# VectorE's order in attention, two moves on TensorE, and the last update in halves, in a two-layer hybrid decoder

## The chip, the cores and the metric

The kernel runs on 1 core of one Trainium2 chip. The time is device microseconds of one launch, the median of several runs. The engines of the core are TensorE (PE, with its weight loads PEld), VectorE (DVE), ScalarE (ACT), GpSimd (POOL) and SyncE (SP), which here issues all DMAs.

## What is computed

Two layers on 256 tokens of width 1024, float32. Each layer projects its normalised input into queries, keys and values for two groups of heads. Group SWA is sliding-window attention with sinks (8 query heads, 2 key/value heads, window 128), group MOBA is, at 256 tokens, plain causal attention (8 heads). A feed-forward part follows.

```python
def hybrid_layer(x, cos, sin, w_in, b_in, w_out, ...):
    h = rms_norm(x, g_attn_pre)
    proj = jnp.einsum('bsd,de->bse', h, w_in) + b_in
    mq, mk, mv, sq, sk, sv = jnp.split(proj, SPLIT_OFFSETS, axis=-1)
    ...
    mo = rms_norm(moba_attention(mq, mk, mv).reshape(b, s, MOBA_WIDTH), g_moba_out)
    so = rms_norm(swa_sink_attention(sq, sk, sv, sinks).reshape(b, s, SWA_WIDTH), g_swa_out)
    mix = jnp.concatenate([mo, so], axis=-1)
    x = x + rms_norm(jnp.einsum('bse,ed->bsd', mix, w_out), g_attn_post)
    h = rms_norm(x, g_ffn_pre)
    f = jax.nn.silu(jnp.einsum('bsd,df->bsf', h, w_gate)) * jnp.einsum('bsd,df->bsf', h, w_up)
    x = x + rms_norm(jnp.einsum('bsf,fd->bsd', f, w_down), g_ffn_post)
    return x
```

Queries and keys of both groups are rotated (`apply_rope`) between projection and attention.

## The kernel before

**Tiles.** The 256 tokens are two tiles of 128 rows, t = 0 and 1. Weights come in blocks of 1 MB (128 x 2048 float32) into three `raw` buffers. Each float32 product is made of three matmuls: every operand is split into a high part and a low part, and PE adds high x high, high x low and low x high. For each block b, ScalarE writes the high part (`hi`, L500), and VectorE the low part (`lo`, L703), a subtraction that reads the raw block and the high part, both in SBUF: 128 x 2048 elements. `after(L, b)` stands for the parts of the block that takes the place of block b: `after(L, 0)` is `lo` of block 4, `after(L, 1)` of block 5, and so on.

**Projections.** Blocks 0 to 8 are the input projection in five column groups, ci = 0 (SWA keys and values, block 0), 1 (SWA queries, blocks 1 and 2), 2 (MOBA keys, blocks 3 and 4), 3 (MOBA queries, 5 and 6), 4 (MOBA values, 7 and 8). On PE, `multiply(L, t, b)` is one block's matmuls for tile t, and `multiply(L, t, b, (0,))` the first half of them. `project(L, ci, t)` on VectorE (L747, for ci = 0 also L745) takes the sum out of its PSUM bank, scales it and adds the bias, into `stage[t]`.

**Rotation.** `rotate(L, ci, t)` on POOL makes six instructions (L422 to L427) of 128 x 256 elements (128 x 64 for ci = 0) that read `stage[t]` and write `roped[t]`. Then `qk(L, ci, t)` on PE transposes `roped[t]` (L1013), and ScalarE keeps the result (`keep_qk`). `roped[t]` exists once for each tile, so a rotation waits for the transposes of the one before on the same tile:

```python
                if ci:
                    b = BANK_OF["qk", ci - 1, t]
                    pool.wait_ge(full[b], HELD[b].done(L, ("qk", ci - 1, t)))
```

POOL does the rotations in the order (0,0), (1,0), (0,1), (1,1), (2,0), (2,1), (3,0), (3,1), with the small steps of a norm between the last ones.

**Attention** runs in three rounds for each group: `scores` (PE, L1038), `maxima` (VectorE, L766 to L775), `exps` (ScalarE), `probs_transposed` (PE, L1013), `keep_probsT` (half on ScalarE, half on VectorE, L788), `values` (PE, L1063), and `normalise` (VectorE, L797 to L799).

**Order.** Every engine has its own program, one list of calls in a fixed order, and the engines meet only through semaphores. On PE the matmuls of the projections lie between the steps of attention, so that PE has work while other engines do theirs. An engine that waits for one step holds up all that stands behind it in its list.

**The end.** In the last layer `update_x(L, 1, 1)` (VectorE, L827) adds the feed-forward result to `x` for tile 1, over all 1024 columns, and SP then stores the tile with one DMA (L367).

Of the kernel before, what the change touches and what calls it, by code (L numbers as in the profile page):

```python
# [22 lines left out]
ALU = mybir.AluOpType  # L23
# [4 lines left out]
T = 2  # L28
# [7 lines left out]
BANK = 512  # L36
# [3 lines left out]
MOBA, SWA = 0, 1  # L40
# [114 lines left out]
BANK_OF = {name: b for b in range(8) for name in HOLDS[b]}  # L155


def trunk(nc, x_in, w_in, b_in, w_out, g_attn_pre, g_attn_post, g_moba, g_swa, sinks_in,
# [4 lines left out]
    with ExitStack() as ctx:  # L163
# [3 lines left out]
        def sem(name):  # L167
            return ctx.enter_context(nc.semaphore(name))
# [76 lines left out]
        rstd_o_ready = sem("rstd_o_ready")  # L245
        o_scaled = sem("o_scaled")
        eps_added = sem("eps_added")
        pool_step = sem("pool_step")
        dve_step = sem("dve_step")

# [28 lines left out]
        def tokens(t):  # L279
            return slice(t * P, (t + 1) * P)  # L280
# [8 lines left out]
        def _(sp):  # L289
# [40 lines left out]
            for L in range(depth):  # L330
# [23 lines left out]
                if L < depth - 1:  # L354
# [7 lines left out]
                    load_sinks(following)  # L362
                    for b in range(RAW + 1):
                        load_block(following, b)
            for t in range(T):
                sp.wait_ge(x_ready, X_READY.done(depth - 1, (1, t)))
                sp.dma_start(out[0, tokens(t), :], x[:, t, :]).then_inc(out_done, 16)  # L367
            sp.wait_ge(out_done, 16 * T)


        @block.gpsimd
# [318 lines left out]
        def _(dve):  # L690
# [15 lines left out]
            def after(L, b):  # L706
                for c in freed_by(b):
                    lo(L, c)
# [114 lines left out]
            def update_x(L, ph, t):  # L823
# [4 lines left out]
                                               x[:, t, :], ALU.mult, ALU.add).then_inc(x_ready, 1)  # L828
                X_READY.tick((ph, t))

            def swiglu(L, c, t):
                n = min(BANK, FF - c * BANK)
                b = BANK_OF["up", c, t]
                dve.wait_ge(full[b], HELD[b].done(L, ("up", c, t)))
                bg = BANK_OF["gate", c, t]
                dve.wait_ge(drained[bg], HELD[bg].done(L, ("gate", c, t)) + 1)
                if c:
                    bt = BANK_OF["ft", c - 1, t]
                    dve.wait_ge(full[bt], HELD[bt].done(L, ("ft", c - 1, t)))
                nc.vector.scalar_tensor_tensor(f[t][:, 0:n], bank[b][:, 0:n], rstd_x[:, t:t + 1], silu[t][:, 0:n],  # L840
                                               ALU.mult, ALU.mult).then_inc(drained[b], 1)
# [10 lines left out]
            for L in range(depth):  # L852
# [4 lines left out]
                loT(L, ("ht", 0, 1, 1))  # L857
                project(L, 0, 1)
                after(L, 0)
                after(L, 1)  # L860
                maxima(L, SWA, 0)
                project(L, 1, 1)
                after(L, 2)
                keep_probsT(L, SWA, 0)
                after(L, 3)
                project(L, 2, 0)
                normalise(L, SWA, 0)
                project(L, 2, 1)
                maxima(L, SWA, 1)
# [3 lines left out]
                maxima(L, SWA, 2)  # L873
                scale_o(L, SWA, 0)
                keep_probsT(L, SWA, 2)
                after(L, 5)
                project(L, 3, 1)
                after(L, 6)
                normalise(L, SWA, 1)
                maxima(L, MOBA, 0)  # L880
# [64 lines left out]
                    lo(L + 1, 1)  # L945
                    lo(L + 1, 2)
                scale_y(L, 1, 1)
                update_x(L, 1, 1)
                if L < depth - 1:
                    dve.wait_ge(x_ready, X_READY.done(L, (1, 1)))  # L950
                    scale_rows(L + 1, 0, 1)
                assert n_step[0] == (L + 1) * PER_LAYER, n_step
# [3 lines left out]
        def _(pe):  # L956
# [59 lines left out]
            def rows(L, ph, t):  # L1016
                pe.wait_ge(rows_ready, ROWS.done(L, (ph, t)))
                for half in range(2):
                    transpose(L, ("ht", ph, t, half), lambda q: y[t][:, half, q * P:(q + 1) * P], 4)
# [66 lines left out]
            for L in range(depth):  # L1086
# [2 lines left out]
                multiply(L, 0, 1)  # L1089
                multiply(L, 0, 2)  # L1090
                rows(L, 0, 1)
                qk(L, 0, 0)
                multiply(L, 0, 3)
                rows_landed(L, 0, 1)
                multiply(L, 1, 0)
                qk(L, 1, 0)
# [27 lines left out]
                probs_transposed(L, SWA, 2, 0)  # L1124
                probs_transposed(L, SWA, 2, 1)
                multiply(L, 1, 6, (1,))
                values(L, SWA, 2, 0)
                values(L, SWA, 2, 1)
                multiply(L, 0, 7)
                qk(L, 3, 0)  # L1130
                multiply(L, 0, 8, (0,))
                scores(L, MOBA, 0)
# [104 lines left out]
```

## Time and profile before

| | us |
|---|---|
| median of 3 runs | 614.69 |
| fastest and slowest of them | 611.95, 614.82 |
| the profiled execution | 615.06 |
| its span, first to last instruction | 613.3 |

| engine | busy us | share of the span |
|---|---|---|
| PE | 587.2 | 96% |
| PEld | 490.9 | 80% |
| DVE | 346.7 | 57% |
| ACT | 284.1 | 46% |
| POOL | 116.9 | 19% |

The times below are microseconds from the start of the span. In a timeline's row the first number is the start and the second the duration, and a bracket at its end tells how long the engine sat idle before it and what it waited for. Neighbouring instructions of a kind are merged into one row with xcount. Layer 0 reaches from the start to about 308, its attention to about 120; layer 1 follows.

### The profile page before, as it was taken

To read this page: it belongs to the slowest core of one execution; us is meant where nothing else is said; L and a number is where in the kernel's file an instruction comes from. 1 tells how busy PE (TensorE), PEld (TensorE's weight loads), DVE (VectorE), ACT (ScalarE), POOL (GpSimd) and SP (SyncE) were. 2 spreads that over 40 slices of the span, in tenths; PEclk is the share of its full clock that TensorE was granted. 3 is DMA by queue.
4 is the path that set the end of the run, shared out by engine and by line. 5 is a ranking of instruction groups with operands and counts; after the bars stand their busy time and mean duration, and the time that the engine had idled before them with its cause. 6 is when DMAs were issued, how large, how long until landed. Compare 5 with 4: busy or idle time off the path is not lost.

```text
span 613.3 us, 7640 instructions
## 1 busy us (share of the span) xinstructions
PE 587.2 (96%) x3004; PEld 490.9 (80%) x3004; DVE 346.7 (57%) x404; ACT 284.1 (46%) x392; POOL 116.9 (19%) x164
## 2 busy tenths in 40 slices
PE   1998999999999999999999899999999999999995
PEld 1987887888888889888888687888888888898884
DVE  3667666676445445354585657749555555442632
ACT  4364445555443453244365555546654444423520
POOL 1539530340000000000153864016000000000000
PEclk9998999999999999999999899999999999999999
DMA  9954334085755561538465723236486556333701
GB/s 309 330 194 158 104 119 151 24 272 197 248 185 169 197 204 70 206 132 319 159 211 195 246 86 138 69 104 206 148 297 207 162 181 207 137 145 130 274 1 68
DMA packets 50628, 106.74 MB, mean 174 GB/s; under 512 B 2720, under 2 KB 9120, under 8 KB 50592
## 3 DMA queue, kind: packets, MB, share of 16 engines
q1 hardware_dynamic: 50592, 106.25, 50.9%
q8 instruction: 24, 0.39, 0.3%
q14 instruction: 12, 0.10, 0.0%
HBM read 105.19 MB, written 1.05 MB: 173 GB/s over the span
## 4 chain that ended last, share of the span: by engine, by line
PE 83%; POOL 5%; DVE 5%; ACT 3%; issue 1%; DMA 1%; POOLq 0%; SPq 0%; ACTq 0%; DVEq 0%
PE bank L999 74%; PE bank L1013 5%; PE bank L1063 2%; POOL work L422 2%; ACT w_h L500 2%; DVE w_l L703 2%; PE bank L1038 1%; POOL work L426 1%; DVE bank L766 1%; DMA gain_a<-in_g_attn_pre 1%; ACT work L549 1%; POOL work L425 1%; POOL work L424 1%; POOL work L423 0%; POOL work L427 0%
## 5 line engine op out<-in xcount | busy, mean ns | idle before, releaser
L703 DVE TENSOR_TENSOR w_l<-raw,w_h 128x2048 fp32r<-128x2048 f32 x92 | 210.5, 2292 | 151.0 <-ACT w_h L500 151.0
L999 PE MATMUL bank<-w_h,actT_h 128*128 128x512 f32 (+1 forms) x624 | 242.2, 388 | 4.8 <-DVE actT_l L715 4.6
L500 ACT ACTIVATE w_h<-raw 128x2048 fp32r<-128x2048 f32 x92 | 176.2, 1917 | 141.0 <-PE bank L999 122.4
L999 PE MATMUL bank<-w_h,actT_l 128*128 128x512 f32 (+1 forms) x624 | 235.4, 377 | 0.0
L999 PE MATMUL bank<-w_l,actT_h 128*128 128x512 f32 (+1 forms) x624 | 234.8, 376 | 0.0
L999 PEld LDWEIGHTS bank<-w_h,actT_h 128*128 128x128 f32 x624 | 119.2, 191 | 27.6 <-issue 7.7
L999 PEld LDWEIGHTS bank<-w_h,actT_l 128*128 128x128 f32 x624 | 119.1, 191 | 21.7
L999 PEld LDWEIGHTS bank<-w_l,actT_h 128*128 128x128 f32 x624 | 119.4, 191 | 18.7
L441 POOL TENSOR_TENSOR norms<-norms,constants 128x1 f32<-128x1 f32 x8 | 6.7, 838 | 346.7 <-ACT work L527 346.7
L1013 PE MATMUL bank<-ident,work 128*128 128x128 f32 x332 | 49.6, 279 | 14.5 <-DVE work L727 7.9
L1013 PEld LDWEIGHTS bank<-ident,work 128*128 128x128 f32 x332 | 40.3, 143 | 23.4 <-issue 7.9
L999 PE MATMUL bank<-w_h,fT_h 128*128 128x512 f32 x160 | 49.8, 392 | 0.0
L999 PE MATMUL bank<-w_l,fT_h 128*128 128x512 f32 x160 | 49.3, 390 | 0.0
L999 PE MATMUL bank<-w_h,fT_l 128*128 128x512 f32 x160 | 49.3, 389 | 0.0
L549 ACT ACTIVATE work<-bank,neg_max 128x128 f32<-128x128 f32 (+1 forms) x64 | 26.0, 426 | 36.0 <-DVE neg_max L770 36.0
L999 PEld LDWEIGHTS bank<-w_h,fT_l 128*128 128x128 f32 x160 | 30.0, 188 | 6.3
L999 PEld LDWEIGHTS bank<-w_l,fT_h 128*128 128x128 f32 x160 | 30.0, 188 | 6.3
L999 PEld LDWEIGHTS bank<-w_h,fT_h 128*128 128x128 f32 x160 | 29.5, 188 | 5.7
L512 ACT ACTIVATE actT_h<-bank 128x512 fp32r<-128x512 f32 (+1 forms) x28 | 15.2, 568 | 36.6 <-PE bank L1013 36.3
L715 DVE TENSOR_TENSOR actT_l<-bank,actT_h 128x512 fp32r<-128x512 f32 (+1 forms) x28 | 17.6, 649 | 24.3 <-ACT actT_h L512 24.3
L422 POOL TENSOR_TENSOR work<-work,cos 128x256 f32<-128x256 f32 (+1 forms) x16 | 19.8, 1240 | 38.5 <-DVE work L747 36.2
L583 ACT ACTIVATE work<-bank,norms 128x512 f32<-128x512 f32 (+1 forms) x24 | 15.4, 652 | 22.3 <-PE bank L999 22.2
(62 smaller groups left out, 375.3 us busy)
## 6 DMA issues: line engine op xcount, KB each, us to landing
raw<-in_w_gate SPq DMA_DIRECT2D x22, 1024.0 KB, 5.2
raw<-in_w_up SPq DMA_DIRECT2D x22, 1024.0 KB, 5.1
raw<-in_w_down SPq DMA_DIRECT2D x22, 1024.0 KB, 5.1
raw<-in_w_in SPq DMA_DIRECT2D x18, 1024.0 KB, 6.9
raw<-in_w_out SPq DMA_DIRECT2D x8, 1024.0 KB, 5.1
bias<-in_b_in SPq DMA_DIRECT2D x8, 256.0 KB, 5.8
x<-in_x SPq DMA_DIRECT2D x2, 512.0 KB, 6.5
gain_a<-in_g_attn_pre SPq DMA_DIRECT2D x2, 512.0 KB, 5.9
```

The lines of the kernel that those rows point to most:

```text
L422: nc.gpsimd.tensor_tensor(dst[:, :, :, 0:half], x1, c, ALU.mult)
L424: nc.gpsimd.tensor_tensor(dst[:, :, :, half:HEAD], x2, c, ALU.mult)
L441: link(L, nc.gpsimd.tensor_tensor(ss_y[:, t, 0:1], ss_y[:, t, 0:1], eps, ALU.add))
L500: nc.scalar.activation(w["h"][:, slot(b), :], raw[:, r, :], ACT.Copy).then_inc(hi_ready, 1)
L512: nc.scalar.activation(dst["h"][:, k:k + nk, tokens(t)], bank[b][:, 0:nk * P].rearrange("p (k n) -> p k n", k=nk), ACT.Copy).then_inc(hiT_ ...
L549: last = nc.scalar.activation(probs[:, j, n * keys:(n + 1) * keys], bank[4 + j][:, n * keys:(n + 1) * keys], ACT.Exp, bias=neg_max[:, g, t ...
L583: nc.scalar.activation(silu[t][:, 0:n], bank[b][:, 0:n], ACT.Silu, scale=rstd_x[:, t:t + 1]).then_inc(drained[b], 1)
L703: nc.vector.tensor_tensor(w["l"][:, slot(b), :], raw[:, slot(b, RAW), :], w["h"][:, slot(b), :].bitcast(F32), ALU.subtract).then_inc(lo_re ...
L715: nc.vector.tensor_tensor(dst["l"][:, k:k + nk, tokens(t)], bank[b][:, 0:nk * P].rearrange("p (k n) -> p k n", k=nk), dst["h"][:, k:k + nk ...
L999: ins = nc.tensor.matmul(bank[BANK_OF[name]][:, 0:n], left[s][:, at + k, tokens(t)], right[r][:, k, c * BANK:c * BANK + n], start=first an ...
L1013: ins = nc.tensor.transpose(out_[:, q * P:(q + 1) * P], src(q), ident[:])
L1063: ins = nc.tensor.matmul(bank[b][:, h * HEAD:(h + 1) * HEAD], probsT[:, j, at:at + P], v[g][:, kb, cols], start=kb == 0, stop=kb == blocks ...
```

## The change

Four edits on two engines, and one at the end. On VectorE, `project(1, 1)` and the maxima of round (SWA, 0) stand ahead of `after(1)` (the low part of block 5), `project(2, 0)` ahead of `after(3)`, and `project(3, 1)` ahead of `after(5)`. On PE, `multiply(0, 3)` stands ahead of `qk(0, 0)`, and the values of round (SWA, 2) behind the first half of `multiply(0, 7)`. In the last layer the update of tile 1 is done in two halves of 512 columns, each with its own store.

```diff
@@ -245,6 +245,7 @@
         rstd_o_ready = sem("rstd_o_ready")
         o_scaled = sem("o_scaled")
         eps_added = sem("eps_added")
+        half_ready = sem("half_ready")
         pool_step = sem("pool_step")
         dve_step = sem("dve_step")
 
@@ -362,10 +363,13 @@
                     load_sinks(following)
                     for b in range(RAW + 1):
                         load_block(following, b)
-            for t in range(T):
-                sp.wait_ge(x_ready, X_READY.done(depth - 1, (1, t)))
-                sp.dma_start(out[0, tokens(t), :], x[:, t, :]).then_inc(out_done, 16)
-            sp.wait_ge(out_done, 16 * T)
+            sp.wait_ge(x_ready, X_READY.done(depth - 1, (1, 0)))
+            sp.dma_start(out[0, tokens(0), :], x[:, 0, :]).then_inc(out_done, 16)
+            for c in range(2):
+                sp.wait_ge(half_ready, c + 1)
+                cols = slice(c * BANK, (c + 1) * BANK)
+                sp.dma_start(out[0, tokens(1), cols], x[:, 1, cols]).then_inc(out_done, 16)
+            sp.wait_ge(out_done, 16 * 3)
 
 
         @block.gpsimd
@@ -828,6 +832,17 @@
                                                x[:, t, :], ALU.mult, ALU.add).then_inc(x_ready, 1)
                 X_READY.tick((ph, t))
 
+            def finish_x():
+
+                name = ("down", 1, 1)
+                b = BANK_OF[name]
+                dve.wait_ge(drained[b], HELD[b].done(depth - 1, name) + 1)
+                dve.wait_ge(rstd_y_ready, R_Y.done(depth - 1, (1, 1)))
+                for c in range(2):
+                    cols = slice(c * BANK, (c + 1) * BANK)
+                    nc.vector.scalar_tensor_tensor(x[:, 1, cols], y[1][:, c, :], rstd_y[:, 1:2], x[:, 1, cols],
+                                                   ALU.mult, ALU.add).then_inc(half_ready, 1)
+
             def swiglu(L, c, t):
                 n = min(BANK, FF - c * BANK)
                 b = BANK_OF["up", c, t]
@@ -857,13 +872,13 @@
                 loT(L, ("ht", 0, 1, 1))
                 project(L, 0, 1)
                 after(L, 0)
+                project(L, 1, 1)
+                maxima(L, SWA, 0)
                 after(L, 1)
-                maxima(L, SWA, 0)
-                project(L, 1, 1)
                 after(L, 2)
                 keep_probsT(L, SWA, 0)
+                project(L, 2, 0)
                 after(L, 3)
-                project(L, 2, 0)
                 normalise(L, SWA, 0)
                 project(L, 2, 1)
                 maxima(L, SWA, 1)
@@ -873,8 +888,8 @@
                 maxima(L, SWA, 2)
                 scale_o(L, SWA, 0)
                 keep_probsT(L, SWA, 2)
+                project(L, 3, 1)
                 after(L, 5)
-                project(L, 3, 1)
                 after(L, 6)
                 normalise(L, SWA, 1)
                 maxima(L, MOBA, 0)
@@ -945,8 +960,10 @@
                     lo(L + 1, 1)
                     lo(L + 1, 2)
                 scale_y(L, 1, 1)
-                update_x(L, 1, 1)
-                if L < depth - 1:
+                if L == depth - 1:
+                    finish_x()
+                else:
+                    update_x(L, 1, 1)
                     dve.wait_ge(x_ready, X_READY.done(L, (1, 1)))
                     scale_rows(L + 1, 0, 1)
                 assert n_step[0] == (L + 1) * PER_LAYER, n_step
@@ -1089,8 +1106,8 @@
                 multiply(L, 0, 1)
                 multiply(L, 0, 2)
                 rows(L, 0, 1)
+                multiply(L, 0, 3)
                 qk(L, 0, 0)
-                multiply(L, 0, 3)
                 rows_landed(L, 0, 1)
                 multiply(L, 1, 0)
                 qk(L, 1, 0)
@@ -1124,9 +1141,10 @@
                 probs_transposed(L, SWA, 2, 0)
                 probs_transposed(L, SWA, 2, 1)
                 multiply(L, 1, 6, (1,))
+                multiply(L, 0, 7, (0,))
                 values(L, SWA, 2, 0)
                 values(L, SWA, 2, 1)
-                multiply(L, 0, 7)
+                multiply(L, 0, 7, (1,))
                 qk(L, 3, 0)
                 multiply(L, 0, 8, (0,))
                 scores(L, MOBA, 0)
```

VectorE in layer 0, from the projection of (0, 1) (its second instruction) to `project(2, 0)`. L747 is a projection, L703 a low part, L770 and L775 the end of the maxima, L788 a copy of transposed probabilities. Before:

```order
14 L747 SCALAR_TENSOR_TENSOR work<-bank0,norms,bias 128x128
15 L703 TENSOR_TENSOR w_l<-raw,w_h 128x2048 x2
...
32 L770 TENSOR_SCALAR neg_max<-top 128x8
33 L775 TENSOR_TENSOR sink_exp<-sinks,neg_max 128x8
34 L747 SCALAR_TENSOR_TENSOR work<-bank1,norms,bias 128x512
35 L703 TENSOR_TENSOR w_l<-raw,w_h 128x2048
36 L788 COPY work<-bank5 128x512
37 L703 TENSOR_TENSOR w_l<-raw,w_h 128x2048
38 L747 SCALAR_TENSOR_TENSOR work<-bank2,norms,bias 128x512
```

And after (L707, L751, L774, L779 and L792 are the same lines):

```order
14 L751 SCALAR_TENSOR_TENSOR work<-bank0,norms,bias 128x128
15 L707 TENSOR_TENSOR w_l<-raw,w_h 128x2048
16 L751 SCALAR_TENSOR_TENSOR work<-bank1,norms,bias 128x512
...
33 L774 TENSOR_SCALAR neg_max<-top 128x8
34 L779 TENSOR_TENSOR sink_exp<-sinks,neg_max 128x8
35 L707 TENSOR_TENSOR w_l<-raw,w_h 128x2048 x2
36 L792 COPY work<-bank5 128x512
37 L751 SCALAR_TENSOR_TENSOR work<-bank2,norms,bias 128x512
38 L707 TENSOR_TENSOR w_l<-raw,w_h 128x2048
```

`project(1, 1)` (out of bank 1) moved from behind the maxima to ahead of them, one low part moved from ahead of the maxima to behind them, where two now stand together, and `project(2, 0)` (out of bank 2) moved ahead of the third.

VectorE later in the layer, around `project(3, 1)`. Before:

```order
66 L788 COPY work<-bank5 128x512
67 L703 TENSOR_TENSOR w_l<-raw,w_h 128x2048
68 L747 SCALAR_TENSOR_TENSOR work<-bank1,norms,bias 128x512
69 L703 TENSOR_TENSOR w_l<-raw,w_h 128x2048
70 L797 TENSOR_TENSOR row_sum<-row_sum,sink_exp 128x8
```

And after:

```order
66 L792 COPY work<-bank5 128x512
67 L751 SCALAR_TENSOR_TENSOR work<-bank1,norms,bias 128x512
68 L707 TENSOR_TENSOR w_l<-raw,w_h 128x2048 x2
69 L801 TENSOR_TENSOR row_sum<-row_sum,sink_exp 128x8
70 L802 RECIPROCAL row_sum<-row_sum 128x8
```

The projection changed places with the low part ahead of it, and the two low parts are neighbours.

PE in layer 0, around the first transpose of rotated keys (the one into bank 6). L1013 is a transpose, L999 a matmul of a block, bank 2 is `multiply(0, 3)`, bank 0 `multiply(1, 0)`. Before:

```order
52 L1013 MATMUL bank5<-ident,work 128x128 x4
53 L1013 MATMUL bank6<-ident,work 128x128
54 L999 MATMUL bank2<-w_h,actT_h 128x512
...
65 L999 MATMUL bank2<-w_h,actT_l 128x512
66 L999 MATMUL bank0<-w_h,actT_h 128x256
```

And after (L1030 is the transpose, L1016 the matmul):

```order
52 L1030 MATMUL bank5<-ident,work 128x128 x4
53 L1016 MATMUL bank2<-w_h,actT_h 128x512
...
64 L1016 MATMUL bank2<-w_h,actT_l 128x512
65 L1030 MATMUL bank6<-ident,work 128x128
66 L1016 MATMUL bank0<-w_h,actT_h 128x256
```

The transpose moved behind the twelve matmuls of `multiply(0, 3)`.

## Rows read from the trace of the kernel before

**Rows 1.** Waits of PE: engine, line, what for, us in total, times, longest.

```profile
PE bank L1013 <- POOL work L427: 5.8, 5, 2.0
```

**Rows 2.** Timeline of layer 0 around `qk(0, 0)` and `qk(1, 0)`, PE and POOL.

```profile
26.23 0.47 PE L999 MATMUL bank<-w_h,actT_h 128*128 128x512 f32 x1
...
29.06 0.28 PE L999 MATMUL bank<-w_h,actT_h 128*128 128x256 f32 x1
...
31.93 0.60 PE L1013 MATMUL bank<-ident,work 128*128 128x128 f32 x4
...
26.61 0.74 POOL L422 TENSOR_TENSOR work<-work,cos 128x256 f32<-128x256 f32 x1 [1.57 <-PE bank L1013]
...
30.21 0.74 POOL L427 TENSOR_TENSOR work<-work 128x256 f32<-128x256 f32 x1
```

**Rows 3.** Timeline of layer 1 at the same place, PE and POOL.

```profile
321.84 0.33 PE L1013 MATMUL bank<-ident,work 128*128 128x128 f32 x1 [0.66 <-POOL work L427]
...
327.66 0.60 PE L1013 MATMUL bank<-ident,work 128*128 128x128 f32 x4
...
322.75 0.74 POOL L422 TENSOR_TENSOR work<-work,cos 128x256 f32<-128x256 f32 x1 [0.96 <-DVE work L747]
```

**Rows 4.** Timeline of layer 0 from the low parts to `qk(1, 1)`, VectorE, POOL, PE.

```profile
35.00 4.62 DVE L703 TENSOR_TENSOR w_l<-raw,w_h 128x2048 fp32r<-128x2048 f32 x2 [2.19 <-ACT w_h L500]
...
42.17 0.75 DVE L747 SCALAR_TENSOR_TENSOR work<-bank,norms,bias 128x512 f32<-128x512 f32 x1
42.84 2.28 DVE L703 TENSOR_TENSOR w_l<-raw,w_h 128x2048 fp32r<-128x2048 f32 x1
...
47.58 2.38 DVE L703 TENSOR_TENSOR w_l<-raw,w_h 128x2048 fp32r<-128x2048 f32 x1 [0.67 <-ACT w_h L500]
...
43.00 2.72 POOL L422 TENSOR_TENSOR work<-work,cos 128x256 f32<-128x256 f32 x1 [8.26 <-DVE work L747]
...
50.50 0.72 POOL L427 TENSOR_TENSOR work<-work 128x256 f32<-128x256 f32 x1
...
37.93 1.16 PE L1038 MATMUL bank<-kT,qT 64*128 64x128 f32 x16
...
41.88 0.27 PE L1013 MATMUL bank<-ident,work 128*128 128x128 f32 x1
...
51.27 1.12 PE L1013 MATMUL bank<-ident,work 128*128 128x128 f32 x4 [1.96 <-POOL work L427]
```

**Rows 5.** Timeline behind attention of layer 0, two adjacent low parts and POOL.

```profile
122.47 4.48 DVE L703 TENSOR_TENSOR w_l<-raw,w_h 128x2048 fp32r<-128x2048 f32 x2
...
122.79 2.01 POOL L441 TENSOR_TENSOR norms<-norms,constants 128x1 f32<-128x1 f32 x1 [1.03 <-ACT work L527]
```

**Rows 6.** Timeline of layer 0 around `project(3, 1)`, VectorE, POOL, PE.

```profile
71.82 2.29 DVE L703 TENSOR_TENSOR w_l<-raw,w_h 128x2048 fp32r<-128x2048 f32 x1
74.03 0.75 DVE L747 SCALAR_TENSOR_TENSOR work<-bank,norms,bias 128x512 f32<-128x512 f32 x1
...
80.41 0.71 POOL L427 TENSOR_TENSOR work<-work 128x256 f32<-128x256 f32 x1
...
72.81 2.00 PE L1063 MATMUL bank<-v_swa,work 128*128 128x64 f32 x16 [0.31 <-ACT work L561]
...
81.18 0.66 PE L1013 MATMUL bank<-ident,work 128*128 128x128 f32 x4 [0.61 <-POOL work L427]
```

**Rows 7.** Busy times by window: window, length, engines, PEclk (granted clock), DMA share, GB/s.

```profile
51.00:54.00 3.00, 2.73 (x9) 2.35 (x10) 1.13 (x3) 0.60 (x1) 2.83 (x5) 0.50 0.86 296
```

**Rows 8.** The chain that ended last, layer 0: start, us, what.

```profile
52.39 2.20 PE bank L999 x6
...
68.85 1.39 PE bank L999 x6
```

**Rows 9.** Timeline of VectorE at the end, the last update.

```profile
608.89 1.28 DVE L827 SCALAR_TENSOR_TENSOR x<-work,norms,x 128x1024 f32<-128x1024 f32 x1 [0.34 <-POOL norms L444]
```

**Rows 10.** Busy times by window at the end; the last column is GB/s.

```profile
611.00:612.00 1.00, 0.00 (x0) 0.00 (x0) 0.00 (x0) 0.00 (x0) 0.00 (x0) 0.50 0.95 389
```

## The prediction, made before the result was known

> **What bounds the kernel now.** I read the page's busy table first: TensorE (PE) is busy in nearly the whole span, so the time is its work plus its gaps. Next the waits of PE: behind the two of the first 15 us, which nothing in the change touches, the largest is on GpSimd (POOL), 5.8 us in five waits, the longest 1.96 [rows 1]. They are waits for rotations. A rotation of (ci, t) is six POOL instructions between VectorE's `project(ci, t)` and PE's transposes `qk(ci, t)`. Then the timelines at these places. All of these waits lie in the attention part of the two layers; in the feed-forward part PE never waits, so whatever PE loses in attention is lost for good, and whatever it gains is gained.
>
> **Part 1, `multiply(0, 3)` ahead of `qk(0, 0)` on PE.** `rotate(1, 0)` may not start before `qk(0, 0)` has read the tile that it overwrites, and `qk(1, 0)` needs its result. In layer 0 the rotation runs from 26.61 to 30.95, and PE comes to `qk(1, 0)` at 31.93, one microsecond after it [rows 2]. The block that is pulled ahead lasts 29.06 - 26.23 = 2.83 us [rows 2]. So the rotation would run from 29.44 to 33.78, while PE has the same work before `qk(1, 0)` and still arrives at 31.93: a new stall of 1.85 us, **+1.85**. In layer 1 PE now waits 0.66 us for the rotation of (0, 0), and that goes: the block's first matmul moves from 321.94 to about 321.0 (0.66 for the wait, 0.1 for the transpose, and the next matmul is issued while the last drains), and 2.83 us later, at 323.85, the matmul behind `qk(0, 0)` starts. In layer 0 POOL starts 0.38 us behind that matmul (26.23 and 26.61), so here at 324.25, and takes the 4.3 us of now. `qk(1, 0)` starts at 328.6 instead of 327.66 [rows 2, 3]: **+0.95**, a stall of 1.6 us behind the 0.66 that is saved. VectorE runs no low part in either stretch, so nothing else hides or lengthens it. Sum +2.8 us.
>
> **Part 2, VectorE at `project(1, 1)`.** Now VectorE computes two low parts (`lo`, L703) from 35.00 to 39.62, then the maxima, and `project(1, 1)` only at 42.17; POOL starts at 43.00 and ends at 51.22, and PE waits 1.96 us [rows 4]. Eight microseconds for work of 4.3: an L703 running beside it held it up twice, the first instruction for 2.72 us instead of 0.70. It ended 0.60 us behind the L703 (43.00 + 2.72 against 42.84 + 2.28), and an L703 that came behind a POOL instruction lost 0.10 us to it (2.38 for 2.28) [rows 4]. After: the projection starts when its matmuls are done, at 38.1; PE starts the scores behind the last of them at 37.93 [rows 4]. POOL gains less from that than it looks, since `rotate(1, 1)` also waits for `qk(0, 1)`, which PE does at 41.88 [rows 4]: it starts at 42.3 instead of 43.0. What changes more is what it meets. The low part that used to lie at 37.3 to 39.6, where POOL was idle, now comes behind the maxima. These start when the scores are there, at 39.1 instead of 39.54, and end 0.43 us sooner: first low part from 41.75 to 44.03, POOL's first instruction until 44.6, second low part (held up by it) until 46.8, POOL's second until 47.4. Then VectorE copies the probabilities and does `project(2, 0)`, 1.3 us in which POOL does its third. The next low part comes at 48.05, the moment of POOL's fourth; whichever is first, the rotation loses 2.2 us again and ends at 52.2 to 52.45. Three low parts in the way instead of two: `qk(1, 1)` at 52.3 instead of 51.27, **+1.1 in each layer, +2.2**. If POOL did not get in between the two adjacent low parts, its first instruction would end at 46.8 and the three that follow unhindered would cancel that: 52.4 again. That it does get in is seen at 122.79, where a POOL instruction of 0.19 us ended 0.05 behind the first of two adjacent L703 [rows 5]. The copy for the values comes 0.5 us later and still ahead of PE. The weights are ready long before use.
>
> [...]
>
> **Part 3, `project(3, 1)` ahead of a low part, and the values later.** The projection's matmuls end at 72.50 (PE's 72.81 less its wait of 0.31) [rows 6], VectorE is free at 71.82, so it can start at 72.55 instead of 74.03. POOL then comes to 73.4, but the low part that VectorE issues at 73.2 is ahead of it: first POOL instruction until 76.1, second low part 75.95 to 78.25, second instruction until 78.85, then four by 0.7 with 0.1 between: 81.75, against 81.12 now [rows 6]. A start 1.5 us sooner is more than paid for by a second blocked instruction: **+0.6 in each layer, +1.2**. The moved values end PE's 0.31 us wait for ScalarE, but PE then only reaches `qk(3, 1)` sooner and waits there: 1.5 us instead of 0.61. Worth nothing, and it costs nothing. `project(2, 0)` ahead of its low part gives nothing either: its rotation queues behind (1, 1) on POOL. None of the moved low parts is late for PE, and the transfers that wait for them have several microseconds left.
>
> **Part 4, the end.** The last update is 1.28 us [rows 9], then comes the store of 512 KB. In halves, VectorE needs about 0.1 more (two instructions of 512 columns, 0.75 each [rows 6], the second starting just before the first ends), and the first half's store runs under the second half. Behind the last write only 256 KB are left, 0.65 us less at 389 GB/s [rows 10]: **-0.5**, between 0 and -0.8.
>
> **Part 5, the clock.** [...] Four transposes took 1.12 instead of 0.60 us [rows 3, 4] and six matmuls 2.20 instead of 1.39 [rows 8]: 1.33 us for one fall. Behind the waits of 0.61 and 0.66 it did not fall. The two new stalls of 1.6 and 1.85 lie nearer to 1.96, so I count a fall for each: **+2.7**, with ends 0 and 3.4 (a fall that lasts a little longer). The stall of 1.5 at `qk(3, 1)` I count at nothing, with a far end of 2.7 for two falls; the longer wait at `qk(1, 1)` has its fall already, a far end of +1.
>
> **Sum.** 2.8 + 2.2 + 1.2 - 0.5 + 2.7 = +8.4 us on the profiled execution's 615.06: 623.5. That execution stands 0.4 above the median of 614.69, so 623.1.
>
> **Rivals.** (A) Faster: the sooner projections win. If a POOL instruction is not held up again and again, but the low parts behind the maxima cost `rotate(1, 1)` no more than 2.6 us in all, it ends before PE comes at 49.3. Then 1.96 and its fall of 1.33 go in both layers, 0.61 and 0.31 as well, while part 1 and its falls stay: 2.8 + 2.7 - 6.6 - 1.8 - 0.5 = -3.4, so 611.3. For it speaks only that the start is sooner; against it both rows of blocked instructions, 43.00 and 122.79 [rows 4, 5]. Chance 0.06. (B) The clock stays up behind the new stalls: +5.7, so 620.4. For it: nothing between 0.66 and 1.96 is in the trace. Chance 0.2. [...] (C) The clock also falls at `qk(3, 1)` and stays down longer at `qk(1, 1)`: +8.4 + 2.7 + 1, so 626.8. Chance 0.15. (D) On VectorE the sooner start and the extra blocking cancel, part 1 alone stands: 2.8 - 0.5 with none to two falls, +2.3 to +5.0, so 617.0 to 619.7. Chance 0.1. That leaves 0.49 for the forecast.
>
> **The numbers.** Predicted 623.1. The range, 618.0 to 627.5, holds the forecast, B, C and half of D, which is just over 8 in 10. About 0.5%, or 3.1 us, is what a measurement of this kernel can tell from no change. Slower by more: forecast, B, C and half of D and a little, 0.84. Within it: the lower half of D and misses of the sum, 0.10. Faster: A, 0.06.
>
> **What would show it.** In the changed kernel's waits of PE, POOL's line should be about 12 us: 1.85 and 1.6 before `qk(1, 0)`, near 3 before `qk(1, 1)`, near 1.5 before `qk(3, 1)`, none before `qk(0, 0)`. On POOL, `rotate(1, 1)` should show three long instructions and `rotate(3, 1)` two. The granted clock should show four low stretches in attention, not two. If `rotate(1, 1)` takes less than 9 us, part 2 is wrong; if PE goes into `qk(1, 0)` without a gap, part 1 is, and with it the sign.

## The result, and the profile after

The changed kernel takes 622.14 us (median of 5 runs, 620.91 to 624.58) against 613.15 for the kernel before (5 runs, 611.95 to 614.82). The ratio is 1.0137, with a 95% interval of 1.0114 to 1.0161: slower. The medians are 9.0 us apart, and the interval of the ratio stands for 7.0 to 9.9 us. The median before is now 613.15 of five runs, where the prediction started from 614.69 of three. The profiled execution took 624.58, its span is 622.8 us, and the one of the kernel before 613.3.

PE's busy time grew by 3.3 us (587.2 to 590.5), about what two more stretches at the low clock cost (below). POOL's grew by 7.3 (116.9 to 124.2), since its held-up instructions count as busy. The rest of the 9.5 us by which the span grew is mostly the waiting of PE for POOL. The waits of PE, of the kernel after (waited for, us in total, times, longest), answering to [rows 1]:

```profile
PE bank L1030 <- POOL work L431: 13.5, 6, 3.5
PE bank L1030 <- DVE work L731: 8.0, 1, 8.0
PE bank L1016 <- DVE actT_l L719: 4.6, 1, 4.6
```

13.5 us in six waits instead of 5.8 in five. Where they are is told by the timeline of PE: before `qk(1, 0)`, `qk(1, 1)` and `qk(3, 1)` of layer 0, and, in the last row, before `qk(1, 0)` of layer 1, answering to the PE rows of [rows 2, 3, 4, 6]. The other two, 3.46 and 1.75 in layer 1, repeat the middle ones.

```profile
34.12 0.66 PE L1030 MATMUL bank<-ident,work 128*128 128x128 f32 x4 [1.61 <-POOL work L431]
...
54.72 1.00 PE L1030 MATMUL bank<-ident,work 128*128 128x128 f32 x4 [3.45 <-POOL work L431]
...
85.42 0.98 PE L1030 MATMUL bank<-ident,work 128*128 128x128 f32 x4 [1.76 <-POOL work L431]
...
334.33 0.66 PE L1030 MATMUL bank<-ident,work 128*128 128x128 f32 x4 [1.46 <-POOL work L431]
```

The first and the last are new: `multiply(0, 3)` no longer covers `rotate(1, 0)`. The wait before `qk(1, 1)` was 1.96 and the one before `qk(3, 1)` 0.61.

The cause of the long one, in the timeline of POOL and VectorE at `rotate(1, 1)` of layer 0, answering to [rows 4]:

```profile
44.53 2.48 POOL L426 TENSOR_TENSOR work<-work,cos 128x256 f32<-128x256 f32 x1 [8.48 <-PE bank L1030]
46.97 2.79 POOL L427 TENSOR_TENSOR work<-work,sin 128x256 f32<-128x256 f32 x1
49.71 0.73 POOL L428 TENSOR_TENSOR work<-work,cos 128x256 f32<-128x256 f32 x1
50.40 2.79 POOL L429 TENSOR_TENSOR work<-work,sin 128x256 f32<-128x256 f32 x1
53.27 0.72 POOL L430 TENSOR_TENSOR work<-work 128x256 f32<-128x256 f32 x1
53.95 0.72 POOL L431 TENSOR_TENSOR work<-work 128x256 f32<-128x256 f32 x1
...
44.12 5.03 DVE L707 TENSOR_TENSOR w_l<-raw,w_h 128x2048 fp32r<-128x2048 f32 x2
...
50.34 2.27 DVE L707 TENSOR_TENSOR w_l<-raw,w_h 128x2048 fp32r<-128x2048 f32 x1
```

Three of the six instructions last 2.5 to 2.8 us instead of 0.7, one for each of VectorE's low parts (L707) beside them. The rotation takes 10.1 us for 4.3 us of work. Before it took 8.2, with two slow instructions: the first one [rows 4] and the fifth, which was this one:

```profile
47.89 2.65 POOL L426 TENSOR_TENSOR work<-work 128x256 f32<-128x256 f32 x1
```

In the changed kernel the first instruction waits for PE's `qk(0, 1)`, no longer for a projection. POOL does get in between the two adjacent low parts: they take 5.03 us together, against 4.48 where POOL had only a tiny instruction to do [rows 5].

The same at `rotate(3, 1)`, with two slow instructions where there was one, answering to [rows 6]:

```profile
77.07 2.71 POOL L426 TENSOR_TENSOR work<-work,cos 128x256 f32<-128x256 f32 x1 [5.48 <-DVE work L751]
79.75 2.78 POOL L427 TENSOR_TENSOR work<-work,sin 128x256 f32<-128x256 f32 x1
```

And the clock, in the busy times by window (window, length, busy us of PE, PEld, DVE, ACT, POOL, then the granted clock, the DMA share and GB/s), answering to [rows 7]:

```profile
34.00:39.00 5.00, 4.88 (x24) 4.12 (x25) 1.76 (x1) 3.79 (x3) 1.83 (x7) 1.00 0.00 0
...
55.00:58.00 3.00, 3.00 (x10) 2.17 (x8) 0.00 (x0) 0.60 (x1) 2.92 (x5) 0.50 0.77 296
...
86.00:89.00 3.00, 3.00 (x9) 2.42 (x9) 0.00 (x0) 2.56 (x14) 0.15 (x1) 0.50 0.17 66
```

The clock does not fall behind the new wait of 1.61 us that ends at 34. It falls behind the wait of 3.45, and once at `qk(3, 1)`, where it did not fall before. Layer 1 repeats this, so there are four low stretches in attention instead of two.

At the end the last update comes in two halves, answering to [rows 9]:

```profile
618.87 1.41 DVE L843 SCALAR_TENSOR_TENSOR x<-work,norms,x 128x512 f32<-128x512 f32 x2 [0.34 <-POOL norms L448]
```

It begins 1.75 us behind ScalarE's last square (at 617.12; before at 607.13 and 608.89, also 1.76). From there to the end of the span it takes 3.9 us against 4.4.

### The profile page after: what moved, and what is told of

Read it like the earlier page. It is cut to its first block, busy times and chain, and to the rows that moved or that the text cites. A ratio compares the mean times of both kernels' runs of the same rounds, so it can differ in the third digit from the quotient of the medians.

```text
span 622.8 us, 7642 instructions
## 1 busy us (share of the span) xinstructions
PE 590.5 (95%) x3004; PEld 493.8 (79%) x3004; DVE 348.2 (56%) x405; ACT 284.5 (46%) x392; POOL 124.2 (20%) x164
## 4 chain that ended last, share of the span: by engine, by line
PE 88%; POOL 7%; DVE 1%; ACT 1%; DMA 1%; issue 0%; POOLq 0%; DVEq 0%; SPq 0%; ACTq 0%
PE bank L1016 78%; PE bank L1030 6%; PE bank L1080 2%; POOL work L427 2%; POOL work L426 2%; PE bank L1055 2%; POOL work L429 1%; ACT w_h L504 1%; DMA gain_a<-in_g_attn_pre 1%; POOL work L430 1%; POOL work L428 1%; POOL work L431 1%; DVE w_l L707 0%; DVE actT_l L719 0%; ACT actT_h L516 0%
## 5 line engine op out<-in xcount | busy, mean ns | idle before, releaser
L707 DVE TENSOR_TENSOR w_l<-raw,w_h 128x2048 fp32r<-128x2048 f32 x92 | 212.1, 2313 | 153.4 <-ACT w_h L504 153.3
L1016 PE MATMUL bank<-w_h,actT_h 128*128 128x512 f32 (+1 forms) x624 | 244.2, 391 | 4.8 <-DVE actT_l L719 4.6
L1016 PE MATMUL bank<-w_h,actT_l 128*128 128x512 f32 (+1 forms) x624 | 236.5, 379 | 0.0
L1016 PE MATMUL bank<-w_l,actT_h 128*128 128x512 f32 (+1 forms) x624 | 236.2, 379 | 0.0
L1016 PEld LDWEIGHTS bank<-w_h,actT_h 128*128 128x128 f32 x624 | 120.3, 193 | 28.0 <-issue 7.9
L1016 PEld LDWEIGHTS bank<-w_h,actT_l 128*128 128x128 f32 x624 | 119.9, 192 | 22.0
L1016 PEld LDWEIGHTS bank<-w_l,actT_h 128*128 128x128 f32 x624 | 120.5, 193 | 18.8
L1030 PE MATMUL bank<-ident,work 128*128 128x128 f32 x332 | 50.4, 281 | 21.8 <-POOL work L431 13.5
L1030 PEld LDWEIGHTS bank<-ident,work 128*128 128x128 f32 x332 | 40.4, 144 | 30.8 <-POOL work L431 14.6
L1016 PE MATMUL bank<-w_h,fT_h 128*128 128x512 f32 x160 | 49.8, 392 | 0.0
L1016 PE MATMUL bank<-w_l,fT_h 128*128 128x512 f32 x160 | 49.3, 390 | 0.0
L1016 PE MATMUL bank<-w_h,fT_l 128*128 128x512 f32 x160 | 49.3, 389 | 0.0
L1016 PEld LDWEIGHTS bank<-w_l,fT_h 128*128 128x128 f32 x160 | 30.0, 188 | 6.3
L1016 PEld LDWEIGHTS bank<-w_h,fT_l 128*128 128x128 f32 x160 | 30.0, 188 | 6.3
L1016 PEld LDWEIGHTS bank<-w_h,fT_h 128*128 128x128 f32 x160 | 29.5, 188 | 5.7
```

The source lines that it names most:

```text
L707: nc.vector.tensor_tensor(w["l"][:, slot(b), :], raw[:, slot(b, RAW), :], w["h"][:, slot(b), :].bitcast(F32), ALU.subtract).then_inc(lo_re ...
L1016: ins = nc.tensor.matmul(bank[BANK_OF[name]][:, 0:n], left[s][:, at + k, tokens(t)], right[r][:, k, c * BANK:c * BANK + n], start=first an ...
L1030: ins = nc.tensor.transpose(out_[:, q * P:(q + 1) * P], src(q), ident[:])
```

## The experiments

Every kernel is compared with the kernel before, run beside it on the same chip. A "fall" is one stretch in which the granted clock is 0.50. The theory: PE loses in two ways, by `multiply(0, 3)` no longer covering a rotation, and by VectorE's low parts that now run beside rotations and hold them up. The rival: the projections taken ahead help, and the loss lies elsewhere. The first five experiments each make one part of the change alone.

**The block first.** The edit, on PE:

```diff
-                qk(L, 0, 0)
                 multiply(L, 0, 3)
+                qk(L, 0, 0)
```

> The kernel before with one edit: multiply(0, 3) ahead of qk(0, 0) on PE. My theory: rotate(1, 0) now ends after PE has come to qk(1, 0); PE waits there 1.6 us in layer 0 and 1.5 us in layer 1 (as in the changed kernel) and no longer 0.66 before qk(0, 0) of layer 1; +1.8 and +0.9, so +2.7 us in all with the clock up, +5.4 if it falls behind both. Rival (the whole loss is in VectorE's order, and what PE loses here it gets back at qk(1, 1), where it waits anyway): no change, within 0.5 us.

Measured 618.34 us, ratio 1.008 (1.0068 to 1.0092), +5.1. Timeline of PE, layer 0, at `qk(1, 0)` and `qk(1, 1)`:

```profile
33.99 0.65 PE L1013 MATMUL bank<-ident,work 128*128 128x128 f32 x4 [1.59 <-POOL work L427]
...
53.37 0.66 PE L1013 MATMUL bank<-ident,work 128*128 128x128 f32 x4 [1.95 <-POOL work L427]
```

The new wait is 1.59 us, in layer 1 it is 1.46, and the wait before `qk(1, 1)` is unchanged: PE gets nothing back there. The rotation starts 2.1 us later (45.11 for 43.00), as all that leads to it does: ScalarE makes the high part behind the result of `qk(1, 0)` (at 35.17 for 33.06), VectorE its low parts behind that (37.11 for 35.00), and `project(1, 1)` comes last. That rules out the rival. The waits make 1.59 + 1.46 - 0.66 = 2.4 us. The other 2.7 is mostly clock, but not where it was expected. There was no fall behind the new waits. All six runs have a mean granted clock of 0.992 or 0.993, which in the profiled executions is that of two falls in attention, while the median of the kernel before is here one of 0.995, that of one fall (last section). A smaller part is that both falls now lie wholly on matmuls, and that the start came 0.26 us later in this execution. Against the profiled execution of the kernel before, which has two falls as well, the span is only 3.2 us longer (616.5 for 613.3).

**VectorE's order of the first round.**

```diff
                 after(L, 0)
+                project(L, 1, 1)
+                maxima(L, SWA, 0)
                 after(L, 1)
-                maxima(L, SWA, 0)
-                project(L, 1, 1)
                 after(L, 2)
                 keep_probsT(L, SWA, 0)
+                project(L, 2, 0)
                 after(L, 3)
-                project(L, 2, 0)
```

> The kernel before with VectorE's order of the first round alone: project(1, 1) and the maxima ahead of one low part, project(2, 0) ahead of another. My theory: three low parts instead of two hold up rotate(1, 1), which ends 1.25 us later in each layer (PE waits 3.2 to 3.5 us instead of 1.96); +2.5 us, as the clock falls there already. Rival (the projections taken ahead do help, and the loss comes from PE's order): PE's wait before qk(1, 1) shrinks by the 0.7 us that the rotation starts sooner, -1.4 us or more.

Measured 617.0 us, ratio 1.0058 (1.0046 to 1.007), +3.8. PE waits 3.45 us before `qk(1, 1)`, as in the whole change, and POOL shows the same three slow instructions. Timeline of POOL, their three rows:

```profile
41.73 2.48 POOL L422 TENSOR_TENSOR work<-work,cos 128x256 f32<-128x256 f32 x1 [7.56 <-PE bank L1013]
44.17 2.79 POOL L423 TENSOR_TENSOR work<-work,sin 128x256 f32<-128x256 f32 x1
...
47.60 2.79 POOL L425 TENSOR_TENSOR work<-work,sin 128x256 f32<-128x256 f32 x1
```

So this part of the loss comes from this reordering. It is 1.3 us more than the 2.5 expected from the waits, and again all six runs have the mean clock of two falls (0.992). The edit also moves `project(2, 0)` ahead of the third low part. No run moves that alone, so its share stays open.

**The projection (3, 1).**

```diff
                 keep_probsT(L, SWA, 2)
+                project(L, 3, 1)
                 after(L, 5)
-                project(L, 3, 1)
                 after(L, 6)
```

> The kernel before with one edit: project(3, 1) ahead of the low part in front of it. My theory: rotate(3, 1) starts 1.5 us sooner, but its first two instructions are both held up and it ends 0.7 us later; PE waits 1.3 to 1.4 us instead of 0.61: +1.4 us for both layers with the clock up, up to +4 if it falls behind that wait. Rival (the sooner start counts): the wait of 0.61 goes, -1.2 us.

Measured 614.64 us, ratio 1.0026 (1.0014 to 1.0038), +1.4. Timeline of POOL, the first two instructions of the rotation, and of PE:

```profile
71.82 2.72 POOL L422 TENSOR_TENSOR work<-work,cos 128x256 f32<-128x256 f32 x1 [4.75 <-DVE work L747]
74.50 2.78 POOL L423 TENSOR_TENSOR work<-work,sin 128x256 f32<-128x256 f32 x1
...
80.19 0.66 PE L1013 MATMUL bank<-ident,work 128*128 128x128 f32 x4 [1.15 <-POOL work L427]
```

PE waits 1.15 us instead of 0.61. This execution had no fall in layer 0, so all times here are earlier than in [rows 6]. Measured from PE's arrival at `qk(3, 1)` (79.04, before 80.57), the rotation starts 1.5 us sooner and ends 0.55 later, as the theory says.

**The end in halves** (the diff of the change, last part, alone).

> The kernel before with the last update and its store in two halves, nothing else. Both theories: -0.5 us (from 5.68 us between the last ScalarE square and the end of the span in the changed kernel against 6.17 before), hardly to be told from none by the times; the stretch from the last square (607.13) to the end of the span is what decides. Rival: two DMAs at the end cost a fixed time each, 0.

Measured 613.51 us, ratio 1.0003 (0.9989 to 1.0017): no difference that the times can tell. The trace has 5.73 us from the last square (605.47) to the end of the span (611.2), against 6.17. The store's time from issue to landing fell from 2.7 to 2.1 us. So -0.4 us is there.

**The values later.**

```diff
+                multiply(L, 0, 7, (0,))
                 values(L, SWA, 2, 0)
                 values(L, SWA, 2, 1)
-                multiply(L, 0, 7)
+                multiply(L, 0, 7, (1,))
```

> The kernel before with one edit: the values of round (SWA, 2) behind the first half of multiply(0, 7) on PE. My theory: PE's wait of 0.31 us for ScalarE goes and turns up again before qk(3, 1), 0.9 us instead of 0.61, since the end of rotate(3, 1) is set by POOL and VectorE: 0 us. Rival: PE keeps the gain, -0.6 us for both layers.

Measured 613.07 us, ratio 0.9988 (0.997 to 1.0007), not told from none. In the trace the wait of 0.31 is gone and PE waits 1.24 us before `qk(3, 1)` instead of 0.61: nothing is left of the gain, and the wait is 0.3 longer than I expected there.

The product of these five ratios is 1.0156, against 1.0137 (1.0114 to 1.0161) for the whole change. Within the intervals the edits account for it.

**The projection ahead, the low parts in place.** This separates the two things that the second experiment did at once.

```diff
                 after(L, 0)
                 after(L, 1)
+                project(L, 1, 1)
                 maxima(L, SWA, 0)
-                project(L, 1, 1)
                 after(L, 2)
```

> The kernel before with project(1, 1) ahead of the maxima, and every low part where it was (blocks 4 and 5 ahead of the maxima). My theory (low parts beside the rotation are what costs, not the order of projection and maxima): the rotation starts at 42.3 instead of 43.0, its first instruction is free, one low part holds up the second, and it ends at about 48.7, ahead of PE; against that the maxima come 0.66 us later and PE waits that much more before the first transposes of the probabilities. -2.6 us in each layer with the clock staying up, so about -5, 608. If the second low part still meets the rotation, only -0.5. Rival (taking the projection ahead of the maxima is itself what made the changed kernel slower, since it delays the exponentials): +1 to +2 us.

Measured 609.58 us, ratio 0.9922 (0.9901 to 0.9943), faster than before, 1.6 above the 608 that I expected. Timeline of POOL and PE:

```profile
42.17 0.73 POOL L422 TENSOR_TENSOR work<-work,cos 128x256 f32<-128x256 f32 x1 [7.54 <-PE bank L1013]
42.86 0.73 POOL L423 TENSOR_TENSOR work<-work,sin 128x256 f32<-128x256 f32 x1
43.55 2.86 POOL L424 TENSOR_TENSOR work<-work,cos 128x256 f32<-128x256 f32 x1
...
47.88 0.74 POOL L427 TENSOR_TENSOR work<-work 128x256 f32<-128x256 f32 x1
...
44.62 0.63 PE L1013 MATMUL bank<-ident,work 128*128 128x128 f32 x4 [1.19 <-ACT work L549]
```

One slow instruction, and the rotation ends at 48.6, ahead of PE. The price is PE's wait of 1.19 us for the exponentials, since the maxima come later (0.86 was expected). Taking the projection ahead was the good half of the edit, and the rest of it, the low part behind the maxima together with `project(2, 0)` ahead of the third one, undid it.

**The second low part waits.** The other way round: everything as before, but the low part that met the rotation's fifth instruction comes later.

```diff
                 keep_probsT(L, SWA, 0)
-                after(L, 3)
                 project(L, 2, 0)
                 normalise(L, SWA, 0)
+                after(L, 3)
```

> The kernel before with the low part of block 7 (after(3)) behind project(2, 0) and normalise(SWA, 0), nothing else moved. My theory: it was the second thing that held up rotate(1, 1); without it the rotation ends near 49.3 instead of 51.22, PE comes to qk(1, 1) at 49.3, the wait of 1.96 us and the fall of the clock behind it go in both layers: -3.3 us each, -6.5 us, 606.6. Rival (the clock falls there anyway, since this stretch has many small matmuls): -3.9 us. Second rival (the wait moves to qk(2, 0), whose rotation is now held up): less than -2 us.

Measured 610.36 us, ratio 0.9937 (0.9914 to 0.996). The wait before `qk(1, 1)` is gone and the clock does not fall (0.998 and 0.999 in all runs), but two small waits for the exponentials of the next round appear. Timeline of PE:

```profile
57.32 0.63 PE L1013 MATMUL bank<-ident,work 128*128 128x128 f32 x4 [0.34 <-ACT work L549]
58.23 1.07 PE L1013 MATMUL bank<-ident,work 128*128 128x128 f32 x8 [0.28 <-ACT work L549]
```

I expected 606.6 and was 3.8 too low. The sum took the clock's fall off twice from 613.1, which is the time of executions with only one, and it had no row for what becomes late next. The postponed low part also now holds up the rotation of (2, 0), whose third instruction takes 2.79 us at 51.08; PE does not wait for that one.

**The low parts narrow.** The direct test of the cause, on the whole change: the order stays, and only the length of three instructions changes. The rest of these low parts is left out of the computation.

```diff
-                nc.vector.tensor_tensor(w["l"][:, slot(b), :], raw[:, slot(b, RAW), :],
-                                        w["h"][:, slot(b), :].bitcast(F32), ALU.subtract).then_inc(lo_ready, 1)
+                c = 64 if b in (5, 6, 7) else BLOCK
+                nc.vector.tensor_tensor(w["l"][:, slot(b), 0:c], raw[:, slot(b, RAW), 0:c],
+                                        w["h"][:, slot(b), 0:c].bitcast(F32), ALU.subtract).then_inc(lo_ready, 1)
```

> The changed kernel, with the low parts of blocks 5, 6 and 7 computed for 64 of 2048 columns only (the rest of these low parts is left out, so part of the product is missing); the order of all instructions is unchanged. My theory (a low part that runs beside a rotation holds up POOL for as long as it lasts): rotate(1, 1) takes 4.4 us instead of 10.1, ends ahead of PE, and PE's wait of 3.45 us before qk(1, 1) goes in both layers with the fall of the clock behind it; -9 to -10 us on the changed kernel's 622.1, so about 612.5. rotate(3, 1), whose low parts are whole, still shows two instructions of 2.7 us. Rival (POOL's slow instructions come from the transfers or from the order of the projections): rotate(1, 1) still takes over 8 us, and the time stays within 2 us of 622.

Measured 610.55 us, ratio 0.995 to the kernel before (0.9931 to 0.9968), 11.6 us below the changed kernel, where 9 to 10 were expected. The two were run at different times, with the kernel before at 613.16 and 613.15 beside them. Timeline of POOL, first and last instruction of `rotate(1, 1)`:

```profile
43.48 0.74 POOL L426 TENSOR_TENSOR work<-work,cos 128x256 f32<-128x256 f32 x1 [8.48 <-PE bank L1031]
...
47.07 0.74 POOL L431 TENSOR_TENSOR work<-work 128x256 f32<-128x256 f32 x1
```

4.3 us instead of 10.1, and no wait before `qk(1, 1)`. In the same execution `rotate(3, 1)`, whose low parts are whole, still has two slow instructions:

```profile
70.84 2.71 POOL L426 TENSOR_TENSOR work<-work,cos 128x256 f32<-128x256 f32 x1 [5.49 <-DVE work L752]
73.52 2.78 POOL L427 TENSOR_TENSOR work<-work,sin 128x256 f32<-128x256 f32 x1
```

The order of the instructions is that of the changed kernel, so at `rotate(1, 1)` the order costs only by what VectorE runs beside POOL. The waits of 1.61 and 1.75 at the other two places are as they were.

**The changed kernel mended in one place.** VectorE's first round as in the experiment of the waiting low part, the rest of the change kept.

> The changed kernel with VectorE's order of the first round put as in e7 (both low parts and the maxima ahead of project(1, 1) again, the low part of block 7 behind normalise), and the changes at multiply(0, 3), project(3, 1), the values and the end kept. My theory: PE's waits of 3.45 us go, those of 1.6 and 1.46 before qk(1, 0) and of 1.76 before qk(3, 1) stay, with at most the falls behind the latter; -6.9 of waits, +0.6 for the new small ones before the probabilities' transposes and -3 of clock: about 613. Rival (the clock's falls only move to the next wait): 616.

Measured 613.16 us, ratio 1.0001 (0.9984 to 1.0017): 9.0 us below the changed kernel, as expected. Its waits of PE:

```profile
PE bank L1030 <- POOL work L431: 6.6, 4, 1.8
...
PE bank L1030 <- ACT work L553: 1.6, 6, 0.3
```

The four waits of 1.45 to 1.76 us are still there, and in the profiled execution (613.00 us, mean clock 0.998) the clock fell behind none of them. Eight of the ten runs have such a mean clock (0.998 or 0.999). The other two have 0.995 and 0.993 and took 615.51 and 616.82.

**A version that is faster than both.** The waiting low part, the later values and the end in halves, and the idea of the waiting low part again at `rotate(3, 1)`. This last part of the edit:

```diff
                 keep_probsT(L, SWA, 2)
+                project(L, 3, 1)
+                normalise(L, SWA, 1)
                 after(L, 5)
-                project(L, 3, 1)
-                after(L, 6)
-                normalise(L, SWA, 1)
                 maxima(L, MOBA, 0)
                 project(L, 4, 0)
                 scale_o(L, SWA, 1)
+                after(L, 6)
```

> e7, and the same idea at rotate(3, 1): project(3, 1) as soon as its matmuls are done, then normalise(SWA, 1), one low part, the maxima, project(4, 0), scale_o, and only then the other low part; the values later as in the changed kernel, and the end in halves. My theory: as e7, and the waits of 0.61 and 0.31 us go in both layers and 0.5 us at the end: -6.5 - 1.8 - 0.5, 604.4. Rival (the postponed low parts delay PE's blocks or the transfers that wait for them): no faster than e7.

Measured 606.95 us, ratio 0.988 (0.986 to 0.9901). The expected 604.4 was 2.5 too low: it was built on the 606.6 expected of the waiting low part alone, which had measured 3.8 more. `rotate(3, 1)` runs free, 4.3 us from 71.29, and PE's waits are:

```profile
PE bank L1030 <- ACT work L553: 1.5, 6, 0.3
PE bank L1030 <- POOL work L431: 0.7, 1, 0.7
```

The last one is that before `qk(0, 0)` of layer 1, for which the change had moved `multiply(0, 3)`. Half the block does it:

```diff
-                qk(L, 0, 0)
-                multiply(L, 0, 3)
+                if L:
+                    multiply(L, 0, 3, (0,))
+                    qk(L, 0, 0)
+                    multiply(L, 0, 3, (1,))
+                else:
+                    qk(L, 0, 0)
+                    multiply(L, 0, 3)
```

> e8, and in layer 1 qk(0, 0) between the two halves of multiply(0, 3) instead of ahead of it: part 1 of the change in a half, where PE did wait. My theory: the wait of 0.65 before qk(0, 0) goes, and rotate(1, 0), which starts 0.3 us later than now, ends 0.1 to 0.3 us after PE has come to qk(1, 0): -0.4 us, 606.5, less than the times can tell; the trace decides. Rival (as with the whole block): PE waits over 1 us before qk(1, 0), +0.5 or more.

Measured 606.63 us, ratio 0.9884 (0.9866 to 0.9901), not told from the one before it by the times. In the trace the wait is gone and no new one has come before `qk(1, 0)`.

## Why the prediction was right

The forecast was +8.4 us, 623.1; measured were +9.0 and 622.14. The waits, the held-up rotations and the end came as forecast. The places and the price of the clock's falls did not. Step by step, from the two profiled executions:

- **Part 1.** Expected +1.85 and +0.95. From the start of the eight transposes ahead (25.33 and 25.73) to `qk(1, 0)` it was 6.60 us before and is 8.39 after, +1.79; in layer 1 (320.15 and 325.95) +0.87. Right, and the first experiment shows it alone. The waits are 1.61 and 1.46, each a little below what I had.
- **Part 2.** Expected +1.1 in each layer. From `qk(1, 0)` to `qk(1, 1)` it was 19.34 and is 20.60, +1.26, and +1.25 in layer 1. Three slow instructions as drawn. The term was 0.15 too small: the first low part behind the maxima came 0.2 later than I had placed it.
- **Part 3.** Expected +0.6 each. From `qk(1, 1)` to `qk(3, 1)` it was 29.91 and is 30.70, +0.79 in layer 0, of which some 0.3 is clock (the fall before began while PE still waited, the one after does not); in layer 1 +0.51. The moved values are worth nothing, as said, by the trace of their own experiment.
- **Part 4.** Expected -0.5; 6.17 us before, 5.68 after, from the last square to the end: -0.49.
- **Part 5.** The number of falls is right, four instead of two, and their places are wrong. The forecast had one measured kind to go by: behind the wait of 1.96 us, which ends at 51.27, the granted clock was 0.50 [rows 7], and it was again behind that of layer 1. I laid the two new ones behind the waits before `qk(1, 0)`; there were none. They came at `qk(3, 1)`, which stood in rival C. The failed step is "the two new stalls of 1.6 and 1.85 lie nearer to 1.96, so I count a fall for each": the length of the wait alone doesn't tell, as the first experiment and the mended kernel show. That the total came out right is in part luck. The price of a fall was low as well. The long stretch from `qk(3, 1)` to the next layer holds one fall in the changed kernel and none before, and is otherwise the same work: 240.53 us for 238.97. In layer 1, from `qk(3, 1)` to the last square, it is 231.46 for 229.90. So one fall costs 1.56 us when PE works through it. My 1.33 was read where PE was still waiting for the first 0.66 us of the fall.
- **The sum of the stretches.** 0.40 (in this execution the start came later), 1.79, 1.26, 0.79 and 1.56 in layer 0, 0.87, 1.25, 0.51 and 1.56 in layer 1, and -0.49 at the end make the 9.5 us by which the span grew.
- **The yardstick.** These two executions are not the middle ones. The one before (615.06) stands 1.9 above its median of five, the one after (624.58) 2.4 above its own, though its mean clock of 0.988 is no lower than the 0.987 of the median run. What those 2.4 us are no trace shows. So the 9.0 between the medians can't be split as finely as the 9.5.

Rival A is ruled out by the rows of the changed kernel, and D by the second and third experiments. B and C each came true by half: the clock stayed up behind the new stalls, as B says, and fell at `qk(3, 1)`, as C says. Their totals, 620.4 and 626.8, did not come, because the two misses of the forecast cancel. The chances of the forecast, B, C and half of D add up to 0.89, not to the "just over 8 in 10" that the prediction gives its range.

The prediction's reading of [rows 5], that a waiting POOL instruction gets in between two adjacent low parts of VectorE, held: in the changed kernel the two took 5.03 us, 0.55 more than the 4.48 there, and POOL's first two instructions beside them took 2.48 and 2.79 us.

## What to carry to other kernels

Before moving a VectorE instruction like the low parts here, look at what POOL does at its new place, not only at who waits for its result: here a low part was free where POOL was idle and cost 2 us of POOL's chain where it was not (an instruction of 0.73 us took 2.79). An earlier start of a chain can be worth nothing if what holds it up moves in as well, so write down which instructions overlap it before and after. And when a block is pulled ahead of a step to fill a wait, count what covered the step behind it; half a block was enough here.

## What was not expected of the hardware

In the 13 executions profiled, the granted clock in attention fell to 0.50 for 3.4 us (in the kernel before, in layer 0, from 50.6 to 54.0) or not at all, and not by the length of the wait alone. Behind 1.96 us it fell in both layers in the profiled executions of the kernel before and of the experiment with the block first, and in one of the two in those of the halves, of the projection (3, 1) and of the later values. Behind 3.45 us it fell in all four cases profiled. Behind 1.75 us before `qk(3, 1)` it fell in the changed kernel, and not in the profiled executions of the mended one and the one with narrow low parts, where the same wait stands at the same place of the program.

Nor does a fall start at a fixed place of the wait. The clock in windows of half a microsecond, first the kernel before in layer 0, where the wait ends at 51.27, then the experiment with the block first, where it ends at 53.37:

```profile
50.50:51.00 0.50, 0.00 (x0) 0.00 (x0) 0.50 (x2) 0.00 (x0) 0.50 (x2) 0.61 0.00 0
...
54.50:55.00 0.50, 0.50 (x3) 0.35 (x3) 0.00 (x0) 0.16 (x1) 0.50 (x2) 0.69 1.05 389
```

The first fall starts while PE still waits, the second over 1 us after PE has gone back to work.

The times of the kernel before come in groups that go with the number of falls. Of the 23 runs beside the first four experiments, the 4 with a mean granted clock of 0.992 took 614.95 to 615.63 us, and the 19 with 0.994 to 0.997 took 612.66 to 613.53. The share of the slower group changes from one set of runs to another: it is 9 of the 17 beside the next four experiments, so that the median there is 614.61, and 5 of the 18 beside the last three. A median of this kernel can move by 1.5 us for this reason alone. The groups lie 2 us apart, a little more than the 1.56 of one fall, and the difference is not explained. What decides a fall beside the length of the wait stays open: no run here sets anything but the wait.
